# New address remainders modulo 512 for six split activation tensors of a two-layer encoder trunk

## The reference, cut to what matters

```python
def reference(x, ...):
    for i in range(2):
        h = rmsnorm(x, mix_norm[i])
        y = swa_sink_attention(h, ...) if i == 0 else gla(h, ...)
        x = x + y
        x = x + conv_ffn(rmsnorm(x, ffn_norm[i]), f_w_up[i], f_conv_w[i], f_conv_b[i], f_w_down[i])
    return rmsnorm(x, final_norm)

def conv_ffn(h, w_up, conv_w, conv_b, w_down):
    u = h @ w_up
    gate, up = u[..., :D_FF], u[..., D_FF:]
    ...                                   # conv: width 3 over tokens, on the gate
    return (jax.nn.silu(conv) * up) @ w_down
```

## Time and profile before

| | us |
|---|---|
| median of 3 runs | 1124.08 |
| lowest and highest | 1123.52, 1124.08 |
| the profiled execution | 1123.7 |
| its span, first to last instruction | 1121.9 |

### The profile page before, as it was taken

One profiled execution on the slowest core, in us unless ns is written; L12 is line 12 of the kernel. 1 busy time (PEld: TensorE's weight loads), 2 busy tenths in 40 slices (PEclk: granted clock), 3 DMA queues, 4 the chain that ended last, 5 costly groups with the idle time before them and its releaser, 6 DMA issues.

```text
span 1121.9 us, 14060 instructions
## 1 busy us (share of the span) xinstructions
PE 1099.9 (98%) x5162; PEld 906.0 (81%) x5162; DVE 577.8 (52%) x734; ACT 484.8 (43%) x707; POOL 160.8 (14%) x123
## 2 busy tenths in 40 slices
PE   6999999999999999999999999999999999999996
PEld 5888778888888888888788888778888888888886
DVE  4588565555555553334354556866455555542214
ACT  6366555444454432222652345454544544431211
POOL 6100021111111110001021221121111111110001
PEclk9999999999999999999999999999999999999998
DMA  6511122222222232221222211222222223332212
GB/s 193 160 65 60 36 99 93 100 100 99 93 93 93 101 128 81 100 96 57 79 87 94 80 43 59 84 96 94 93 93 93 93 98 106 108 104 104 84 71 76
DMA packets 31622, 103.48 MB, mean 92 GB/s; under 512 B 3873, under 2 KB 8641, under 8 KB 31586
## 3 DMA queue, kind: packets, MB, share of 16 engines
q1 hardware_dynamic: 27680, 100.68, 26.2%
q10 hardware_dynamic: 3906, 2.31, 1.1%
HBM read 99.56 MB, written 2.88 MB: 91 GB/s over the span
## 4 chain that ended last, share of the span: by engine, by line
PE 89%; DVE 5%; ACT 3%; DMA 1%; POOL 1%; issue 1%; SPq 0%; DVEq 0%; POOLq 0%
PE PS L315 78%; DVE WL L1006 2%; PE PS L636 1%; PE PS L362 1%; PE PS L415 1%; POOL SS L1350 1%; ACT WH L678 1%; PE PS L433 1%; DVE X L1031 1%; ACT SQ L708 1%; PE PS L423 1%; DMA X<-xT 1%; PE PS L547 1%; PE PS L579 0%; PE PS L566 0%
## 5 line engine op out<-in xcount | busy, mean ns | idle before, releaser
L315 PE MATMUL PS<-XH,WH 128*128 128x512 f32 x992 | 393.9, 397 | 9.9 <-DVE XL L1024 9.8
L315 PE MATMUL PS<-XH,WL 128*128 128x512 f32 x992 | 387.2, 390 | 0.0
L315 PE MATMUL PS<-XL,WH 128*128 128x512 f32 x992 | 386.9, 390 | 0.0
L1006 DVE TENSOR_TENSOR WL<-WRAW,WH 128x1024 fp32r<-128x1024 f32 (+1 forms) x169 | 228.9, 1355 | 242.5 <-ACT WH L747 72.0
L315 PEld LDWEIGHTS PS<-XH,WH 128*128 128x128 f32 x992 | 186.7, 188 | 53.5 <-issue 11.8
L315 PEld LDWEIGHTS PS<-XH,WL 128*128 128x128 f32 x992 | 186.6, 188 | 39.6
L315 PEld LDWEIGHTS PS<-XL,WH 128*128 128x128 f32 x992 | 186.8, 188 | 39.2 <-issue 1.7
L1360 POOL TENSOR_TENSOR CV<-CV,R 128x512 f32<-128x512 f32 x44 | 70.5, 1603 | 416.7 <-ACT CV L724 416.7
L315 PE MATMUL PS<-AH,WH 128*128 128x512 f32 x308 | 119.8, 389 | 0.0
L315 PE MATMUL PS<-AL,WH 128*128 128x512 f32 x308 | 119.8, 389 | 0.0
L315 PE MATMUL PS<-AH,WL 128*128 128x512 f32 x308 | 119.8, 389 | 0.0
(11 more groups left out here) (204 smaller groups left out, 1206.3 us busy)
## 6 DMA issues: line engine op xcount, KB each, us to landing
WRAW<-w_up SPq DMA_DIRECT2D x88, 512.0 KB, 3.2
WRAW<-w_down SPq DMA_DIRECT2D x32, 704.0 KB, 4.0
WRAW<-w_bin SPq DMA_DIRECT2D x24, 512.0 KB, 3.2
WRAW<-w_qkv SPq DMA_DIRECT2D x11, 512.0 KB, 4.7
WRAW<-w_o SPq DMA_DIRECT2D x7, 512.0 KB, 3.6
WRAW<-w_bo SPq DMA_DIRECT2D x7, 512.0 KB, 3.3
X<-xT SPq DMA_DIRECT2D x4, 512.0 KB, 6.7
out<-X SPq DMA_DIRECT2D x5, 256.0 KB, 2.2
```

Source lines behind the costliest of these rows:

```text
L315: last = mm(PS[:, bank], w[:, c:c + P], x[:, kb], start=start and n == 0 and w is wh and x is hi, stop=stop and n == len(kbs) - 1 and w is wl)
L1006: tt(WL[:, s, 0:k * P], WRAW[:, s, 0:k * P], WH[:, s, 0:k * P].bitcast(F32), ALU.subtract)\
```

## The change

A table gives six tensors a distance that is added to the common remainder: AH and YH lie 32 bytes behind it, AL, OH and OL 256, and YL 384. XH, XL, WH, WL and the buffers of the fifth units are not in the table.

```diff
 ROW, PHASE = 512, 128
+BEHIND = {"AH": 32, "AL": 256, "OH": 256, "OL": 256, "YH": 32, "YL": 384}
...
             if at is None and dt == F32R:
-                place_at[0] += (PHASE - place_at[0]) % ROW
+                place_at[0] += (PHASE + BEHIND.get(name, 0) - place_at[0]) % ROW
...
-        y_at = place_at[0] + (PHASE - place_at[0]) % ROW
+        y_at = place_at[0] + (PHASE + BEHIND["YH"] - place_at[0]) % ROW
         YH = place("YH", [P, KT_D, T], F32R)
         YL = place("YL", [P, KT_D, T], F32R)
         GT = place("GT", [P, 4, 2, T], at=y_at)
```

## The result

| | before | after |
|---|---|---|
| median us | 1123.8 (4 runs, 1123.39 to 1124.08) | 1129.93 (4 runs, 1129.75 to 1130.81) |
| span of the profiled execution | 1121.9 | 1128.1 |

The changed kernel is slower by 6.1 us. The ratio is 1.0055 with a 95% interval of 1.0043 to 1.0067, so the loss is small but beyond the scatter of the executions.

A forecast was written before the change was run, and what follows sets the result against it. TensorE was taken to bound the kernel, matmul count times pitch; the profiled execution's 1123.7 us plus nothing for addresses or neighbours gave a forecast of 1124.0 us, range 1114 to 1136, with no change at 0.50.

The forecast's parts named there:

- The bound: Whole kernel: TensorE, busy 98% of the span, sets the time as number of matmuls times a pitch of 226.7 ns.
- The count: Matmuls on the path: 990 wide and 132 narrow in down products (A), 83 and 85 in output projections (O, Y); 1290.
- the 107 that I had called covered: Second output projection, reading YH and YL: 107 of 192 matmuls lie off the path, a 5 ns pitch rise hidden by waiting.
- The neighbours: GS, CV and AC moving by 256 bytes, and engines writing the six tensors elsewhere, were costed at nothing.
- Between -15.0 and +10.7 us I take zero: On the 1290 path matmuls: the new remainders' cost, bounded by a 15.0 us gain and 10.7 us loss, taken as zero.
- constant of 32 cycles: Every fp32r matmul, wide or narrow: about 13.3 ns above streaming time, read as a fixed weight-change cost rather than a collision.
- the unsettled pitch: Matmuls behind a wait, 168.35 to 170.43 us: 231.1 ns each, worst two 235; if lasting, 5.7 or 10.7 us lost.
- The slower rival: Down products first: unequal remainders keep streams unsettled, 231.1 ns giving 1129.4 us or 235 ns giving 1134.4 us; chance 0.30.
- The faster rival: The 1290 path matmuls: the 32 cycles are collisions that distance removes, 1108.7 us in full, 1119 for a third; chance 0.20.
- The bound of 4 cycles from the float32 matmuls: Line 566: float32 matmuls spend 1.7 ns changing weights; matching this would win 11.6 ns a matmul, 15.0 us in all.
- Two reads that are said not to meet: TensorE: the skill's pages give independent weight and activation read ports and reads without waiting, so addresses can't matter; sum zero.
- The test by OH and OL: Output projection: OH and OL, sharing a remainder, against AH and AL tell whether distance to weights or between activations matters.

The follow-up runs named there:

- run 4: Against the changed kernel: AH and AL both at 256 bytes, OH 32, OL 384, YH 32, YL 256; 1124.03 us.
- run 11: Against the changed kernel: XH also at 32 and XL at 256, AH and AL kept, OH, OL, YH, YL at 0; 1139.88 us.
- run 3: Against the changed kernel: high and low parts equal, AH and AL at 32 bytes, OH and OL 64, YH and YL 128; 1130.2 us.
- Run 10: Against the changed kernel: all activations back at 0, WRAW and WL 32 bytes behind WH, fifth units' buffers unmoved; 1147.86 us against 1123.33 before.

## Why the prediction was wrong, point by point

**The bound.** Right: the time is the number of matmuls times the pitch. The whole loss stands in the chain as pitch, and VectorE's waits before it writes AL are unchanged.

**The count.** The 990 wide matmuls of A carry 990 x 6.67 ns = 6.6 us, against 6.1 measured in all. The 85 of Y carry 0.4 us, and the 107 that I had called covered are: from the end of the piece of 60 to the next long piece pass 32.04 us, 32.07 before. The 83 of O carry nothing, because 256 is as good as 0, which no row of before could show. The 132 narrow ones have the other sign, some 0.3 us less; I had given them the same constant as the wide ones.

**The neighbours.** Right: run 4 has GS, CV and AC where the change has them and took 1124.03 us against 1123.82.

**The step that failed** is "Between -15.0 and +10.7 us I take zero". I rested it on a constant of 32 cycles that is the same for X, A, O and Y and for both widths, and on the missing step where X gives way to A. All of these have equal remainders. They are one measurement, repeated, at the one distance where nothing was to be seen; that they agree says that the tensor doesn't matter, not that its address doesn't. The runs put 6.7 ns in place of that zero on each of the 990 wide matmuls of the down products (233.3 against 226.7), 4.4 ns on Y and nothing on O. The row that did bear on the question was the unsettled pitch, which shows that the cost depends on how the streams fall against each other. I had read it so, and then given it too little weight: 0.30 for slower where 0.50 went to no change. (The "worst two" of the earlier trace rows are 230 and 236 ns in the trace, 233 on average; the two from 168.58 us on, 234 and 235, are the pair that its 235 fits.)

**The slower rival** was true, with time and place: 1129.4 us at a pitch of 231.1, measured 1129.93, and the loss in the down products. Its mechanism was right in one half. The relation of the two reads does set the pitch, if not alone (run 11). But nothing "stays unsettled", and a change of relation at every matmul isn't needed: run 3, with both parts at 32, is as slow. Nor does it cost by itself: (0, 256) has it and is at 226.7 ns. It can add to the cost, for (0, 64), (64, 0) and (64, 320) are 3 to 4 ns above (64, 64). The near hit of the price is luck: only Y was at the 4.4 ns of the sum, and 6.7 on A, 0 on O and less than 0 on the narrow ones nearly make up for each other.

**The faster rival** is out for all 20 pairs tried that hold a distance other than 0 and 256: every one is at 228.9 ns or more in the wide matmuls. (What reads X is two thirds of the fp32r matmuls, 2976 of 4482, and not the three quarters of the text.) The bound of 4 cycles from the float32 matmuls was no price for this. Where the 32 cycles at equal remainders come from, these runs don't tell.

**Two reads that are said not to meet.** The Trainium skill, page "SBUF — State Buffer", section "SBUF: two separate sides", lets TensorE's reads wait for nobody. Run 10 differs: an unchanged stream of activations lost 6.7 ns a matmul when one weight load in three was moved by 32 bytes. The measurement decides. The 2.5 ns of the Trainium skill, page "TensorE: Matmul & The Clock Gate", section "Wait — 56ns, not 53.3ns?", were reached by no fp32r matmul here: the lowest settled value is 13.3 ns over the 213.3 of 512 columns, and 10.0 over the 106.7 of 256.

**The tests that I had named.** The one by pitch worked. The 33 matmuls of line 363 were to take 7.48, 7.63 or more, or 7.10 us; they took 7.70. "I am wrong if the pitch in any of the three products differs by more than 2 ns" was met in two of them. The test by OH and OL did not work: at 256 bytes from the weights they lost nothing, which would have said that the difference between the two activations is what matters. Run 3 shows that it is not needed.

## What to carry to other kernels

Where TensorE bounds a kernel with one weight load to each fp32r matmul of 512 columns, the remainder of the activations' addresses against the weights' is a tuning parameter: equal, or 256 bytes apart, was best in every place tried, and 32 bytes of displacement cost up to 3% of a matmul. At 256 columns equal remainders were not the best (below). Give both one remainder and keep it when a tensor is inserted ahead of them. And when rows of a profile agree about something that none of them varies, count them as one row.

## What the runs showed of the hardware that was not expected

- The settled pitches of wide fp32r matmuls lie for the most part on steps of 2.2 ns: 226.7, 228.9, 231.1, 233.3. Three matmuls take 680, 686.7, 693.3 or 700 ns. Some lie off them (231.7, 232.0, 232.3, 234.3).
- One and the same pair of distances has more than one rhythm: (32, 256) at 233.3 ns behind a settled X at 0, at 231.1 behind an X at (32, 256).
- Narrow matmuls (256 columns) mostly go the other way: 120.0 ns at (0, 0) and (256, 256), 117.7 at (32, 256), 116.7 at (32, 32) and (288, 288), but 118.3 at (224, 224) and still 120.0 at (96, 96). No kernel was tried that displaces the narrow ones and leaves the wide ones at 0.
- With AL alone displaced by 128 bytes, the matmul that streams it takes 234 ns and its two neighbours stay at 226 and 226.7. Why two reads meet at all, and why the rhythms differ, these runs don't tell.
- The period of 256 bytes holds for 0, 32 and 64 and nearly for 128, each tried with high and low part equal, but not for the mixture (64, 320), which is 4.2 ns slower than (64, 64). Whether this is the address or again the history was not tried.
